# The last norm's token tiles 0 and 1 moved from VectorE to ScalarE and GpSimd

## The chip, the cores and the metric

One NeuronCore of a Trainium2 chip. The metric is the device time of one execution in microseconds (us); before and after are each the median of several runs.

## What is computed

One inference step of a two-layer backbone on 512 latent tokens (`x_sample`) and 128 context tokens (`x_prompt`), 1024 features each. Every layer ends with a squared-ReLU MLP, a gated residual sum and a layer norm; the last of these norms gives the two token outputs:

```python
def layer_norm(x, g, b):
    mu = jnp.mean(xf, -1, keepdims=True)
    var = jnp.mean(jnp.square(xf - mu), -1, keepdims=True)
    return (xf - mu) * lax.rsqrt(var + LN_EPS) * g + b
...
fl = sq_relu_mlp(modulate(xl, ml[3], ml[4]), p["w_up"], p["w_down"])
xl = layer_norm(ALPHA * xl + ml[5] * fl, p["ln2_g"], p["ln2_b"])   # and xc for the prompt
```

## The kernel before

The tokens stand on the partitions in five tiles of 128 (`NT` = 5): tiles 0 to 3 are the latent tokens (`LAT` = 4), tile 4 the prompt. `x[:, t, :]` (named x_tok in the profile) holds tile t as 128x1024 fp32, `acc` a scratch tile of the same shape, `gb` the norm's scale and bias, spread over all partitions, `lnve`, `lnmv` and `lnrs` (ln_small) one or a few numbers per token. Each engine runs its own program in order; semaphores tie them.

The end of the kernel is the last down projection. Its last step makes ten groups, each 12 products of 128x128 by 128x512 into one PSUM bank: `LAST` names them as (half of the features, tile): (0,0), (0,1), (1,0), (1,1), (0,2), (1,2), (0,3), (0,4), (1,3), (1,4). For each group `last_group` (VectorE) multiplies the bank with the gate (one input in PSUM, one in SBUF) and adds the product to `x` (both inputs in SBUF). `LAST_FREE` lets PE reuse a bank only once VectorE's product of an earlier group has been taken: group 8 needs that of group 4, group 9 that of group 5.

When both halves of a latent tile are added, VectorE signals `x_sum`, and `moments` on ScalarE takes the sum of the tile, its negative mean and the sum of the squared deviations (three activations, the first and the last with an accumulator read). `norm_share(3)` on GpSimd scales that sum, adds epsilon and takes the power -0.5 (one element per partition each), which signals `ln_rs`. VectorE applies the norm in two passes per tile, both with two SBUF inputs: `centred` writes (x - mean) * g into `acc`, `final` writes acc * rstd + b into `x` and signals `ln_x`. In the loop over the ten groups they are called for tile 0 after group 4, for tile 1 after group 5, for tile 2 after group 7. After group 9 follow the prompt tile's statistics (`stats`, on VectorE), then `centred(3)`, `centred(4)`, `final(3)` and `final(4)` in two halves. SyncE stores the tiles in the order 0 to 4, each when its `ln_x` has come.

The three norms before this one use `normed` on ScalarE: x * rstd - mean * rstd in place, one activation with `lnrs[:, t, 0:1]` as scale and `lnrs[:, t, 1:2]` as bias.

Of the kernel before, what the change touches and what calls it, by code (L numbers as in the profile page):

```python
# [15 lines left out]
ALU = mybir.AluOpType  # L16
# [6 lines left out]
NT = 5  # L23
LAT = 4
# [88 lines left out]
def build(nc, A, O):  # L113
# [21 lines left out]
    with ctx:  # L135
# [11 lines left out]
        def sem(name):  # L147
            return ctx.enter_context(nc.semaphore(name))
# [10 lines left out]
        x = at("x_tok", 48, [P, NT, D])  # L159
# [6 lines left out]
        gb = at("ln_gb", 184, [P, 2, D])  # L166
# [105 lines left out]
        def two(b, n=HALF):  # L272
# [50 lines left out]
        gb_ld = sem("gb_ld")  # L323
        x_sum, x_mean = sem("x_sum"), sem("x_mean")

        ln_st, ln_rs, ln_n, ln_x, ln_tr, ln_ma, ln_lo = (sem(n) for n in
            ("ln_stat", "ln_rsd", "ln_n", "ln_x", "ln_tr", "ln_ma", "ln_lo"))
# [7 lines left out]
        ic_ld = [sem("ic_ld0"), sem("ic_ld1")]  # L335
        vs, ss_ = sem("dve_step"), sem("pool_step")
        fin, fin2 = sem("stores"), sem("stores_pool")

        (x_prompt, x_sample, cache_k, cache_v, state_ssm, c_in, c_ctx) = (
            A[n] for n in ("x_prompt", "x_sample", "cache_k_l0", "cache_v_l0", "state_ssm_l0", "c", "c_ctx"))  # L340
# [183 lines left out]
        @block.sync  # L524
        def _(sp):
            def load(k, i=None):

                if k == THIRD_K:
                    sp.wait_ge(ib_mm, 8 * NT)
                if k == POOL_K + 1:  # L530
                    sp.wait_ge(acc_ok, DOWNS)
                if k == MIX_K + 2:
                    sp.wait_ge(acc_pre[0], 2)
                if k == w_k[W_OUT[1] + 1]:
                    sp.wait_ge(pl_lo, KT)
                j = raw_before(k)
                if j >= 0 and S[j][0] == "mod":
                    sp.wait_ge(mod_main, m_ord[j] + 1)
                elif j >= 0:
                    sp.wait_ge(lo_done, lin(OPS[w_ord[j] + 1], PER, i))  # L540
                kind, layer, n = S[k]
                if kind == "up":
                    c0 = n * BW if i is None else bass.ds(i * (4 * BW) + n * BW, BW)
                    src = A[f"w_up_l{layer}"][:, slice(c0, c0 + BW) if i is None else c0]
                elif kind == "down":
                    r0 = (n // 2) * CHUNK
                    rows = slice(r0, r0 + CHUNK) if i is None else bass.ds(i * (2 * CHUNK) + r0, CHUNK)
                    src = A[f"w_down_l{layer}"][rows, (n % 2) * 512:(n % 2) * 512 + 512]
                elif kind == "out":
                    src = A[f"w_out_l{layer}"][(n % 2) * 512:(n % 2) * 512 + 512, (n // 2) * 512:(n // 2) * 512 + 512]  # L550
                elif kind == "pool":
                    src = A["pool_w_l1"].rearrange("g k n -> (g k) n")
                elif kind == "mod":
                    src = A[f"w_mod_l{layer}"][:, n * BW:(n + 1) * BW]
                else:
                    src = A[f"w_{kind}_l{layer}"][:, n:n + BW]
                src = src.rearrange("(k p) n -> p k n", p=P)
                sp.dma_start(raw_block(k).rearrange("p (k n) -> p k n", n=src.shape[2]), src) \
                    .then_inc(raw_ld[raw_slot(k)], 16)

            sp.dma_start(head[:], A["t_head"]).then_inc(ld_head, 16)
            sp.dma_start(vec_rows[0:8, 0, :], A["c"].rearrange("a (k p) -> (a k) p", p=P)).then_inc(ld_vec, 16)
            sp.dma_start(vec_rows[8:16, 0, :], A["c_ctx"].rearrange("(k p) -> k p", p=P)).then_inc(ld_vec, 16)
            sp.dma_start(vec_rows[16:56, 0, :], A["conv_w_l0"].rearrange("j (k p) -> (j k) p", p=P)).then_inc(ld_vec, 16)
            sp.dma_start(vec_rows[56:64, 0, :], A["conv_b_l0"].rearrange("(k p) -> k p", p=P)).then_inc(ld_vec, 16)
            sp.dma_start(vec_rows[64:72, 0, :], A["pool_scale_l1"].rearrange("(k p) -> k p", p=P)).then_inc(ld_vec, 16)
            for l in range(2):
                sp.dma_start(vec_rows[48 * l:48 * l + 48, 2, :],
                             A[f"b_mod_l{l}"].rearrange("(k p) -> k p", p=P)).then_inc(ld_vec, 16)
            k = 0  # L570
            for layer in range(2):
                while k < K_UP[layer] + PRE:
                    load(k)
                    k += 1
                with sp.Fori(0, 2) as i:
                    for j in range(BODY):
                        load(k + j, i)
                k += 2 * BODY
            while k < NS:
                load(k)  # L580
                k += 1
            for t in range(LAT):
                sp.wait_ge(ln_x, 3 * NT + t + 1)
                sp.dma_start(y_sample[0, t * P:(t + 1) * P, :], x[:, t, :]).then_inc(fin, 16)
            for n in range(2):
                sp.wait_ge(ln_x, 3 * NT + LAT + n + 1)
                sp.dma_start(y_prompt[0][:, n * 512:(n + 1) * 512], x[:, LAT, n * 512:(n + 1) * 512]).then_inc(fin, 16)
            sp.wait_ge(fin, 16 * (NT + 1))

# [2 lines left out]
        def _(pool):  # L592
# [4 lines left out]
            steps = [0]  # L597
# [91 lines left out]
            def load_gb(i):  # L689
# [3 lines left out]
                for n, which in enumerate("gb"):  # L693
                    pool.dma_start(gb[:, n, :], A[f"ln{half + 1}_{which}_l{layer}"].partition_broadcast(P)) \
                        .then_inc(gb_ld, 16)

            def norm_share(i):

                for t in range(NT):
                    if i == 3 and t < LAT:  # L700
                        pool.wait_ge(x_mean, 3 * t + 3)
                    else:
                        pool.wait_ge(ln_st, NT * i + (t if i < 3 else 0) + 1)
                    if i == 3 and t < LAT:
                        pool.tensor_scalar(lnve[:, t, 1:2], lnve[:, t, 1:2], 1.0 / D, EPS, ALU.mult, ALU.add).then_inc(ss_, 1)
                        steps[0] += 1
                        pool.wait_ge(ss_, steps[0])
                    power = pool.tensor_tensor(lnrs[:, t, 0:1], lnve[:, t, 1:2], halfp[:, 0:1], ALU.pow)
                    if i == 3:
                        power.then_inc(ln_rs, 1)  # L710
                        continue
                    power.then_inc(ss_, 1)
                    steps[0] += 1
                    pool.wait_ge(ss_, steps[0])
                    pool.tensor_tensor(lnrs[:, t, 1:2], lnve[:, t, 0:1], lnrs[:, t, 0:1], ALU.mult).then_inc(ln_rs, 1)

            def spill_x(layer):

# [683 lines left out]
        def _(act):  # L1402
# [472 lines left out]
            def moments(t):  # L1875

                act.wait_ge(x_sum, t + 1)
                act.activation(tmp[:, 0, :], x[:, t, :], ACT.Copy, accum_out=lnmv[:, t, 0:1]).then_inc(x_mean, 1)
                act.wait_ge(x_mean, 3 * t + 1)
                act.activation(lnve[:, t, 0:1], lnmv[:, t, 0:1], ACT.Copy, scale=-1.0 / D).then_inc(x_mean, 1)  # L1880
                act.wait_ge(x_mean, 3 * t + 2)
                act.activation(tmp[:, 1, :], x[:, t, :], ACT.Square, bias=lnve[:, t, 0:1],
                               accum_out=lnve[:, t, 1:2]).then_inc(x_mean, 1)

            for t in range(LAT):
                moments(t)


        @block.vector
        def _(dve):  # L1890
# [513 lines left out]

            def centred(t):

                if t == 0:
                    dve.wait_ge(gb_ld, 32 * 4)
                if t < LAT:
                    dve.wait_ge(x_mean, 3 * t + 2)  # L2410
                else:
                    settle()
                mark(dve.scalar_tensor_tensor(acc[:, t, :], x[:, t, :], lnve[:, t, 0:1], gb[:, 0, :], ALU.add, ALU.mult))

            def final(t):

                dve.wait_ge(ln_rs, NT * 3 + t + 1)
                settle()
                for n in range(2 if t == LAT else 1):
                    cols = slice(n * 512, (n + 1) * 512) if t == LAT else slice(0, D)  # L2420
                    dve.scalar_tensor_tensor(x[:, t, cols], acc[:, t, cols], lnrs[:, t, 0:1], gb[:, 1, cols],
                                             ALU.mult, ALU.add).then_inc(ln_x, 1)
# [127 lines left out]
            def mlp(layer):  # L2550
# [39 lines left out]
                if layer == 1:  # L2590
                    for n in range(2 * NT):
                        last_group(layer, n)
                        if n in (4, 5, 7):
                            centred((4, 5, 7).index(n))
                            final((4, 5, 7).index(n))
                    stats(3, LAT)
                    centred(3)
                    centred(LAT)
                    final(3)
                    final(LAT)  # L2600
                    return
# [139 lines left out]
```

## Time and profile before

| | |
|---|---|
| median of 3 runs | 1454.09 us (1453.24 to 1454.53) |
| the profiled execution, its own time | 1453.4 us |
| its span, first to last instruction | 1451.6 us |
| busy share of the span | PE 96%, VectorE 72%, ScalarE 37%, GpSimd 5% |
| granted TensorE clock, mean | 0.993 of full speed |

In the profile PE is TensorE's products, PEld its weight loads, DVE is VectorE, ACT ScalarE, POOL GpSimd, SP SyncE. A row of the timeline has start in us from the span's start, duration in us, engine, line, operation, output<-inputs, shapes and count; in brackets stands how long the engine was idle before it and what ended that. Rows with a count above 1 are merged neighbours. A start may lie a little before the end of the instruction ahead of it.

### The profile page before, as it was taken

Reading aid. Unit: us, or ns where it says so; the run is one execution under the profiler, and the core shown is the slowest. Engines: PE = TensorE matmul, PEld = TensorE weight load, DVE = VectorE, ACT = ScalarE, POOL = GpSimd, SP = SyncE. Lnnn points to the kernel's source line nnn. Section 1 sums busy time; section 2 is a strip of 40 time slices with the busy share of each in tenths; the row PEclk is TensorE's granted clock in tenths of the full one; section 3 lists DMA queues with packets and bytes.
Section 4 is the critical chain, followed back from the end, with each engine's and each line's share of the span. In section 5 each row is a group of like instructions: output and inputs, shape, how many; then the busy total and the mean of one; then the engine's idle time right before and its main releaser. Section 6 shows DMA issues by size and latency. Waiting matters only on the chain.

```text
span 1451.6 us, 22838 instructions
## 1 busy us (share of the span) xinstructions
PE 1399.1 (96%) x8806; PEld 1241.4 (86%) x8806; DVE 1040.4 (72%) x1651; ACT 543.1 (37%) x982; POOL 77.4 (5%) x146
## 2 busy tenths in 40 slices
PE   4999999899999999999999999999999999999996
PEld 3899988656788998998998879887999899889985
DVE  3694566577568976776776796967887677667778
ACT  3333443267535432332332243434443233223322
POOL 1300000010200000000000111000100000000011
PEclk8999999999999999999999999999999999999998
DMA  9701234496713422312221723551332222123141
GB/s 317 228 30 59 88 118 132 152 333 223 273 58 104 144 60 87 116 59 79 95 87 58 247 82 103 187 194 58 131 116 66 81 87 88 58 87 114 56 163 73
DMA packets 132300, 177.47 MB, mean 122 GB/s; under 512 B 4170, under 2 KB 104258, under 8 KB 131698
## 3 DMA queue, kind: packets, MB, share of 16 engines
q1 hardware_dynamic: 123250, 146.46, 31.5%
q0 software_dynamic: 7376, 26.76, 5.3%
q10 hardware_dynamic: 1584, 3.01, 0.5%
q8 instruction: 61, 1.00, 0.3%
q14 instruction: 29, 0.24, 0.1%
HBM read 166.94 MB, written 9.27 MB: 121 GB/s over the span
## 4 chain that ended last, share of the span: by engine, by line
PE 80%; DVE 10%; ACT 5%; issue 2%; DMA 2%; ACTq 0%; POOL 0%; SPq 0%; DVEq 0%
PE ps L789 40%; PE ps L1307 20%; PE ps L771 6%; PE ps L780 4%; PE ps L820 3%; DVE convT L2002 2%; DVE wlo L1906 1%; PE ps L1115 1%; ACT h_full L1702 1%; DVE p_pad L2669 1%; ACT tmp L1702 1%; ACT whi L1412 1%; PE ps L1126 1%; ACT e_att L1622 1%; DMA raw<-in_w_mod_l 1%
## 5 line engine op out<-in xcount | busy, mean ns | idle before, releaser
L1412 ACT ACTIVATE whi<-raw 128x512 fp32r<-128x512 f32 (+2 forms) x193 | 178.6, 935 | 357.8 <-PE ps L789 293.5
L789 PE MATMUL ps<-whi,hid_hi 128*128 128x512 f32 x640 | 249.6, 390 | 0.0
L789 PE MATMUL ps<-wlo,hid_hi 128*128 128x512 f32 x640 | 249.2, 389 | 0.0
L789 PE MATMUL ps<-whi,hid_lo 128*128 128x512 f32 x640 | 249.0, 389 | 0.0
L1906 DVE TENSOR_TENSOR wlo<-raw,whi 128x512 fp32r<-128x512 f32 (+2 forms) x193 | 204.9, 1070 | 26.0 <-ACT whi L1412 22.5
L2335 DVE TENSOR_TENSOR acc<-acc,ps 128x512 f32<-128x512 f32 x120 | 80.2, 683 | 122.0 <-PE ps L789 122.0
L789 PE MATMUL ps<-whi,h_hi 128*128 128x256 f32 (+1 forms) x480 | 157.4, 328 | 2.4 <-DVE wlo L1906 1.4
L789 PE MATMUL ps<-whi,h_lo 128*128 128x256 f32 (+1 forms) x480 | 152.9, 319 | 0.0
L789 PE MATMUL ps<-wlo,h_hi 128*128 128x256 f32 (+1 forms) x480 | 152.8, 318 | 0.0
L789 PEld LDWEIGHTS ps<-whi,hid_hi 128*128 128x128 f32 x640 | 120.1, 188 | 25.3 <-DVE wlo L1906 0.8
L789 PEld LDWEIGHTS ps<-whi,hid_lo 128*128 128x128 f32 x640 | 120.2, 188 | 25.1
L789 PEld LDWEIGHTS ps<-wlo,hid_hi 128*128 128x128 f32 x640 | 120.1, 188 | 24.3
L1307 PE MATMUL ps<-t_hi,whi 128*128 128x320 f32 x384 | 118.7, 309 | 0.0
L1307 PE MATMUL ps<-t_hi,wlo 128*128 128x320 f32 x384 | 118.7, 309 | 0.0
L1307 PE MATMUL ps<-h_lo,whi 128*128 128x320 f32 x384 | 118.6, 309 | 0.0
L1307 PE MATMUL ps<-h_hi,whi 128*128 128x320 f32 x384 | 118.2, 309 | 0.0
L2475 DVE TENSOR_TENSOR tmp<-tmp,ps 128x320 f32<-128x320 f32 x168 | 79.2, 483 | 37.3 <-PE ps L1307 33.1
L789 PEld LDWEIGHTS ps<-whi,h_hi 128*128 128x128 f32 x480 | 91.2, 190 | 10.7 <-issue 2.3
L789 PEld LDWEIGHTS ps<-whi,h_lo 128*128 128x128 f32 x480 | 91.3, 190 | 6.4
L789 PEld LDWEIGHTS ps<-wlo,h_hi 128*128 128x128 f32 x480 | 91.4, 190 | 5.9
L1307 PE MATMUL ps<-h_hi,wlo 128*128 128x320 f32 x288 | 89.0, 309 | 0.0
L771 PE MATMUL ps<-h_hi,whi 128*128 128x320 f32 x320 | 74.3, 314 | 0.0
(339 smaller groups left out, 2657.2 us busy)
## 6 DMA issues: line engine op xcount, KB each, us to landing
raw<-in_w_up_l SPq DMA_DIRECT2D x32, 1024.0 KB, 5.6
raw<-in_w_down_l SPq DMA_DIRECT2D x32, 1024.0 KB, 5.1
raw<-in_w_mod_l SPq DMA_DIRECT2D x26, 1024.0 KB, 5.4
raw<-in_w_in_l SPq DMA_DIRECT2D x12, 1024.0 KB, 5.3
raw_split<-in_w_mod_l SPq DMA_DIRECT2D x8, 1024.0 KB, 7.2
raw<-in_w_out_l SPq DMA_DIRECT2D x6, 1024.0 KB, 5.7
x_spill<-x_tok POOLq DMA_DIRECT2D x10, 512.0 KB, 2.9
x_tok<-x_spill POOLq DMA_DIRECT2D x10, 512.0 KB, 6.1
```

Of the source, the lines that this page charges most:

```text
L771: mm = pe.matmul(outs[hf], w_of(still, k), a_of(part, k, hf), start=(k == 0 and part == 0 and still == 0), stop=(k == nk - 1 and still == 1))
L780: mm = pe.matmul(out, w_of(still, k), a_of(part, k, hf), start=(k == 0 and part == 0 and still == 0), stop=(k == nk - 1 and still == 1))
L789: mm = pe.matmul(out, a_of(still, k), w_of(part, k), start=(first and k == 0 and part == 0 and still == 0), stop=(last and k == nk - 1 and ...
L820: mm = pe.matmul(ps[32 * g:32 * g + 32, lo:lo + BW], cpad[:, k, :], raw_block(mod_k[m])[:, k * BW:(k + 1) * BW], start=(k < 4), stop=(k >= 4))
L1115: mm = pe.matmul(bank(2 * n + part, 0, keys.shape[-1]), qT[r:r + DH, 2 * n + hp, t * P:(t + 1) * P], keys, start=True, stop=True)
L1307: mm = pe.matmul(bank(b, 0, HALF), WP[still][:, pos // 4, lo:lo + P], moving(part, k), start=(k == 0 and still == 0 and part == 0), stop=( ...
L1412: act.activation(ring_piece(whi, w, g), piece(w, g), ACT.Copy).then_inc(hi_done, 1)
L1702: ins = act.activation(dst, bank(TURN[i % 2][t][f // 4], (f % 4) * P, (f % 4 + 1) * P), ACT.Identity, bias=modT[:, layer, q, f, c:c + 1], ...
L1906: dve.tensor_tensor(ring_piece(wlo, w, g), piece(w, g), ring_piece(whi, w, g).bitcast(F32), ALU.subtract).then_inc(lo_done, 1)
L2002: ins = dve.scalar_tensor_tensor(dst, src, tap, dst, ALU.mult, ALU.add)
L2335: dve.tensor_tensor(dst, dst, bank(4 + g % 4), ALU.add).then_inc(acc_ok, 1)
L2475: dve.tensor_tensor(dst, a, bank(b, 0, HALF), ALU.add).then_inc(comb, 1)
```

## The change

For tiles 0 and 1 of the last norm the two VectorE passes go. ScalarE runs `normed(3, 0)` and `normed(3, 1)` among its moments, and GpSimd, inside `norm_share(3)`, makes the negative mean times rstd for them and multiplies and adds `gb` to the whole tile (`closing`), `closing(0)` behind tile 1's small operations and `closing(1)` behind tile 2's power. The stores of tiles 0 and 1 wait for `y_pool` in place of `ln_x`. Tiles 2, 3 and 4 keep their two VectorE passes.

```diff
             for t in range(LAT):
-                sp.wait_ge(ln_x, 3 * NT + t + 1)
+                if t < 2:
+                    sp.wait_ge(y_pool, t + 1)
+                else:
+                    sp.wait_ge(ln_x, 3 * NT + t - 1)
                 sp.dma_start(y_sample[0, t * P:(t + 1) * P, :], x[:, t, :]).then_inc(fin, 16)
...
+            def closing(t):
+
+                if t == 0:
+                    pool.wait_ge(gb_ld, 32 * 4)
+                pool.wait_ge(ln_n, NT * 3 + t + 1)
+                pool.tensor_tensor(x[:, t, :], x[:, t, :], gb[:, 0, :], ALU.mult).then_inc(ss_, 1)
+                steps[0] += 1
+                pool.wait_ge(ss_, steps[0])
+                pool.tensor_tensor(x[:, t, :], x[:, t, :], gb[:, 1, :], ALU.add).then_inc(y_pool, 1)
...
                     power = pool.tensor_tensor(lnrs[:, t, 0:1], lnve[:, t, 1:2], halfp[:, 0:1], ALU.pow)
-                    if i == 3:
+                    if i == 3 and t >= 2:
                         power.then_inc(ln_rs, 1)
+                        if t == 2:
+                            closing(1)
                         continue
                     power.then_inc(ss_, 1)
                     steps[0] += 1
                     pool.wait_ge(ss_, steps[0])
                     pool.tensor_tensor(lnrs[:, t, 1:2], lnve[:, t, 0:1], lnrs[:, t, 0:1], ALU.mult).then_inc(ln_rs, 1)
+                    if i == 3 and t == 1:
+                        closing(0)
...
-            for t in range(LAT):
-                moments(t)
+            moments(0)
+            moments(1)
+            normed(3, 0)
+            moments(2)
+            normed(3, 1)
+            moments(3)
...
                         last_group(layer, n)
-                        if n in (4, 5, 7):
-                            centred((4, 5, 7).index(n))
-                            final((4, 5, 7).index(n))
+                        if n == 7:
+                            centred(2)
+                            final(2)
```

## Rows read from the trace of the kernel before

**Rows 1.** The page, part 1: busy time, share and instructions of each engine.

```profile
PE 1399.1 (96%) x8806; PEld 1241.4 (86%) x8806; DVE 1040.4 (72%) x1651; ACT 543.1 (37%) x982; POOL 77.4 (5%) x146
```

**Rows 2.** Chain that ended last, 1415 to 1452: start, duration, what.

```profile
1417.06 8.47 PE ps L789 x36
```

**Rows 3.** Timeline of PE, products of the last groups: first and last of 61.

```profile
1425.13 0.39 PE L789 MATMUL ps<-whi,hid_lo 128*128 128x512 f32 x1
...
1438.73 0.39 PE L789 MATMUL ps<-whi,hid_lo 128*128 128x512 f32 x1
```

**Rows 4.** Timeline of VectorE, 1425 to the end.

```profile
1425.56 0.69 DVE L2354 TENSOR_TENSOR gated<-ps,gate 128x512 f32<-128x512 f32 x1 [0.85 <-PE ps L789]
1426.28 0.69 DVE L2357 TENSOR_TENSOR x_tok<-x_tok,gated 128x512 f32<-128x512 f32 x1
1426.89 1.28 DVE L2413 SCALAR_TENSOR_TENSOR acc<-x_tok,ln_small,ln_gb 128x1024 f32<-128x1024 f32 x1
1428.28 1.28 DVE L2421 SCALAR_TENSOR_TENSOR x_tok<-acc,ln_small,ln_gb 128x1024 f32<-128x1024 f32 x1
1429.49 0.68 DVE L2354 TENSOR_TENSOR gated<-ps,gate 128x512 f32<-128x512 f32 x1
...
1433.40 0.69 DVE L2354 TENSOR_TENSOR gated<-ps,gate 128x512 f32<-128x512 f32 x1
...
1437.43 1.28 DVE L2421 SCALAR_TENSOR_TENSOR x_tok<-acc,ln_small,ln_gb 128x1024 f32<-128x1024 f32 x1
...
1440.68 0.69 DVE L2357 TENSOR_TENSOR x_tok<-x_tok,gated 128x512 f32<-128x512 f32 x1
1441.41 1.29 DVE L2367 BATCH_NORM_STATS2 ln_small<-x_tok 128x6 f32<-128x512 f32 x2
...
1443.10 2.59 DVE L2413 SCALAR_TENSOR_TENSOR acc<-x_tok,ln_small,ln_gb 128x1024 f32<-128x1024 f32 x2
1445.80 2.61 DVE L2421 SCALAR_TENSOR_TENSOR x_tok<-acc,ln_small,ln_gb 128x1024 f32<-128x1024 f32 x3
```

**Rows 5.** Tile view of the stored tiles, 1419 to 1452: min/median/max ns, starts.

```profile
L587 SPq DMA_DIRECT2D out<-x_tok x2: 332/332/333, 1447.8 to 1448.4; - x2
DMA to landing us min/median/max: 2.6/2.6/2.7
```

**Rows 6.** Source view of L1687: the earlier norms' `normed`, min/median/max ns.

```profile
L1687 ACT ACTIVATE x_tok<-x_tok,ln_small x15: 1242/1244/1281, 421.8 to 1024.6; 128x1024 f32<-128x1024 f32 x15
```

**Rows 7.** Timeline of ScalarE: start of tile 0's moments, end of tile 1's.

```profile
1423.42 1.06 ACT L1878 ACTIVATE tmp<-x_tok 128x1024 f32<-128x1024 f32 x1 [9.69 <-DVE x_tok L2357]
...
1428.44 0.19 ACT L1882 ACTIVATION_READ_ACCUMULATOR tmp<-x_tok,ln_small 128x1 f32 x1
```

**Rows 8.** GpSimd's groups by form: busy us, mean ns, idle before.

```profile
L745 POOL MEMSET u_pad<- 128x1344 f32 x1 | 1.2, 1222 | 0.0
...
L593 POOL MEMSET cpad<- 128x256 f32 x1 | 0.3, 311 | 0.3 <-POOLq L2727 0.3
```

**Rows 9.** Timeline of GpSimd and VectorE in the first norm, around 444.

```profile
444.38 0.67 POOL L715 TENSOR_TENSOR ln_small<-ln_small 128x1 f32<-128x1 f32 x1
...
444.30 0.69 DVE L2324 SCALAR_TENSOR_TENSOR x_tok<-x_tok,gated 128x512 f32<-128x512 f32 x1
444.91 2.28 DVE L1906 TENSOR_TENSOR wlo<-raw,whi 128x2048 fp32r<-128x2048 f32 x1
```

**Rows 10.** Timeline of GpSimd in the last norm.

```profile
1426.45 0.95 POOL L708 TENSOR_TENSOR ln_small<-ln_small,smisc 128x1 f32<-128x1 f32 x1
1428.72 0.90 POOL L705 TENSOR_SCALAR ln_small<-ln_small 128x1 f32<-128x1 f32 x1 [1.31 <-ACT tmp L1882]
1429.70 0.55 POOL L708 TENSOR_TENSOR ln_small<-ln_small,smisc 128x1 f32<-128x1 f32 x1
1433.68 0.19 POOL L705 TENSOR_SCALAR ln_small<-ln_small 128x1 f32<-128x1 f32 x1 [3.43 <-ACT tmp L1882]
...
1443.10 1.69 POOL L708 TENSOR_TENSOR ln_small<-ln_small,smisc 128x1 f32<-128x1 f32 x2
```

More of the change, by code:

```diff
@@ L337, in build @@
         fin, fin2 = sem("stores"), sem("stores_pool")
+        y_pool = sem("y_pool")
         (x_prompt, x_sample, cache_k, cache_v, state_ssm, c_in, c_ctx) = (
@@ L582, in _ @@
             for t in range(LAT):
-                sp.wait_ge(ln_x, 3 * NT + t + 1)
+                if t < 2:
+                    sp.wait_ge(y_pool, t + 1)
+                else:
+                    sp.wait_ge(ln_x, 3 * NT + t - 1)
                 sp.dma_start(y_sample[0, t * P:(t + 1) * P, :], x[:, t, :]).then_inc(fin, 16)
             for n in range(2):
-                sp.wait_ge(ln_x, 3 * NT + LAT + n + 1)
+                sp.wait_ge(ln_x, 3 * NT + LAT + n - 1)
                 sp.dma_start(y_prompt[0][:, n * 512:(n + 1) * 512], x[:, LAT, n * 512:(n + 1) * 512]).then_inc(fin, 16)
@@ L2405, in centred @@
             def centred(t):
-                if t == 0:
+                if t == 2:
                     dve.wait_ge(gb_ld, 32 * 4)
```

## The prediction

> **What bounds the kernel now.** I read the busy line and the last link of PE's work first: PE is busy for 96% of the span [rows 1], so nothing that VectorE saves ahead of PE's last product is worth anything, and only the end of the run is open to this edit. Then the chain that ended last, for the stretch in which it leaves PE: it runs on PE until 1425.5 and on VectorE from there to the end [rows 2]. Then the timeline, engine by engine.
>
> PE's last product ends at 1438.73 + 0.39 = 1439.12 [rows 3]. Each of the ten last groups is 12 products, and the 60 from 1425.13 to 1438.73 give 0.227 each, so a group comes every 2.72. VectorE took group 4 at 1425.56, having waited 0.85 for PE [rows 4]; so the groups are ready for it at 1425.56, 1428.28, 1431.00, 1433.72, 1436.44 and 1439.16. It doesn't follow that beat: the two passes over tile 0 (`centred` at 1426.89, `final` at 1428.28) push group 5 to 1429.49 [rows 4], 1.2 behind PE, and with those of tiles 1 and 2 the add of group 9 starts at 1440.68 and ends at 1441.37 [rows 4]. Without any of these passes group 9 would be taken at 1439.16 and its add would end at 1440.57 (0.69 + 0.03 + 0.69). So VectorE's lateness behind PE is worth 0.80 us at most. Behind that add everything is serial on VectorE: statistics of the prompt tile from 1441.41, two `centred` from 1443.10, three `final` pieces from 1445.80 [rows 4], and the last store issued at 1448.4, landing 2.7 later [rows 5]. The edit leaves this tail as it is, 10.2 us behind the last add.
>
> **The change, part by part.** All the steps are put on the time line of before, and the sum is how far the end of group 9's add moves from 1441.37.
>
> *Removed from VectorE:* two passes on tiles 0 and 1. From the start of `centred` at 1426.89 to the next group at 1429.49 a pair takes 2.60 [rows 4], so 5.2 us of work goes. By the 0.80 above at most 0.8 of it can show: the rest was cover for waiting on PE.
>
> *Added to ScalarE:* two `normed` of 1.244 [rows 6]. ScalarE's `moments` of tile 0 runs from 1423.42, and tile 1's ends at 1428.44 + 0.19 = 1428.63 [rows 7]; then `normed(0)` runs to 1429.85. `moments(2)` can't start before group 5's add ends (1428.28 + 1.41 = 1429.69), so it runs 1429.8 to 1432.4 (2.6, half of the 5.21 that two took), and `normed(1)` to 1433.65. This is hidden: before, the scale behind tile 2's moments began as late as 1433.68 [rows 10].
>
> *Added to GpSimd:* a small multiply for tiles 0 and 1 (0.2 to 0.7, like the one at 444.38 [rows 9]), and in `closing(0)` and `closing(1)` four 128x1024 operations with two SBUF inputs. GpSimd is in order, so tile 2's `power`, on which VectorE's `final(2)` waits, now stands behind `closing(0)`, and those of tiles 3 and 4 behind `closing(1)`. No row of before has a wide GpSimd operation with inputs. The nearest are its memsets: 1.222 for 1344 elements and 0.311 for 256 [rows 8], 0.84 ns an element, so 0.95 for 1024 that are only written: the lower bound. If two reads and a write pass one after another it is three times that, less two starts of 0.1: about 2.7, the upper bound. Two reads in turn with the write beneath give 1.8. I take the middle of the last two, 2.25, because each of the streams needs at least the memset's time and something is lost in joining them. The Trainium skill (GPSIMD Engine Reference, 3.1 Elementwise) has 4497 ns for 2048 elements of such an add; half of it is 2.25, and no run here shows it yet.
>
> *The wait between the two engines.* GpSimd's one-element operations show a pattern [rows 9, 10]. The multiply at 444.38 took 0.67, and ended 0.06 behind VectorE's 444.30 + 0.69, an operation with both inputs in SBUF. The scale at 1428.72 took 0.90 and ended at 1429.62, 0.06 behind the end of `final` (1429.56), again two SBUF inputs. The scale at 1433.68 took 0.19, though VectorE was at work, on a group's product with one input in PSUM (from 1433.40 [rows 4]). So there is a way into SBUF which a two-input VectorE operation needs, and GpSimd stands still for the whole of it. I assume the other direction too: a wide GpSimd operation that holds it makes VectorE's two-input operations wait to its end. The rows can't show that, since GpSimd's operations there need the way only for one element. The multiply at 444.38 also shows who is next: the second VectorE operation (444.91, two inputs) was queued as well and GpSimd still got in between, so I let the two engines alternate.
> The Trainium skill (SBUF — State Buffer, Who interferes with whom) says the same of both directions: a VectorE operation with two SBUF inputs and a GpSimd one that reads SBUF exclude each other, the first to issue keeps the shared pair and the other fully blocks. It speaks against this edit: by it the sum below is +4.2, with only the direction that the rows show it is -0.6.
>
> The working, with 2.25 for a wide operation:
> - `power` and multiply of tile 1, ready from 1428.63, finish between 1429.9 and 1430.4, as its `power` meets group 5's add (1429.00 to 1429.69) or not; `closing(0)` multiply 1430.2 to 1432.45.
> - VectorE group 6: product 1431.00 to 1431.69, its add (two inputs) wants 1431.72, gets 1432.45, ends 1433.14.
> - `closing(0)` add: 1433.14 to 1435.39.
> - Group 7: product 1433.72 to 1434.41; add gets 1435.39, ends 1436.08. `centred(2)` 1436.00 to 1437.28 (1.28).
> - GpSimd: scale of tile 2 slips in at 1436.1, `power` waits for `centred(2)` and ends 1437.28 + 0.43 = 1437.71 (0.43 is what the `power` at 1426.45, 0.95 long, took beyond the add that ended at 1426.97 [rows 4, 10]).
> - Now `final(2)` and `closing(1)`'s multiply want the way at once. GpSimd's next instruction needs no signal from another engine, so I give it the turn: 1437.8 to 1440.05. `final(2)` 1440.05 to 1441.33.
> - `closing(1)` add 1441.33 to 1443.58. Group 8: product done by 1441.94, add 1443.58 to 1444.27. Group 9: product 1444.19 to 1444.88, add 1444.91 to 1445.60.
>
> 1445.60 - 1441.37 = **+4.2 us**. Group 8's product starts at 1441.25, 4.8 after PE was done with it. Behind it no wide GpSimd operation is left. The `power` of tiles 3 and 4 keeps its place: before, both were done (1443.10 + 1.69 = 1444.79 [rows 10]) 1.0 ahead of `final(3)`, and they hang on the same adds as before. Stores: tile 1's starts at 1443.7 and tile 2's right behind it, in the same queue; at 2.6 to 2.7 to landing each, both are through before tile 3's (1451.4) and cost nothing. PE isn't touched: its groups 8 and 9 need the banks of groups 4 and 5, freed long before.
> The profiled execution took 1453.4 with a span of 1451.6; that becomes 1457.6. The median of the runs is 0.7 above that execution, so 1454.1 + 4.2 = **1458.3**.
>
> With the operation's time the sum moves about fourfold, for all four stand in the chain: at 1.8 the same working gives +2.4, at 1.9 about +2.9, at 2.7 +6.0. At the memset's 0.95 nearly everything fits into PE's beat, and it gives +0.3.
>
> **Rivals.**
> - *VectorE wins the turn at 1437.8.* `final(2)` runs to 1439.03, `closing(1)` multiply to 1441.28, group 8's add to 1441.97, the last GpSimd add to 1444.22, group 9's add to 1444.91: +3.5, 1457.6. Close to the forecast in kind; no row measures who wins when both become ready together.
> - *VectorE doesn't wait for GpSimd* (not slower). Its adds go through, GpSimd alone waits: `closing(0)` ends at 1434.8, scale at 1435.18, `power` behind `centred(2)` at 1436.75, `final(2)` to 1438.1, and group 9's add ends at 1440.8: -0.6, 1453.5. For it: no row shows VectorE held. Against it: each row of the other direction shows waiting for the whole, no sharing. It decides as soon as an add of VectorE beside a wide operation keeps its 0.69. A quick wide operation (under 1.9) gives "no change" too, +0.3 to +2.9.
> - *Wide operations longer than 2.7*, since each takes its inputs in turn and the engine's program costs something per element. At 3.2 the fourfold gives +8, 1462. Nothing in the profile speaks for it but that small operations of this engine aren't quick (0.55 for one element of `power`).
>
> **How the numbers follow.** Under 0.2% (2.9 us) this kernel's runs can't be told from no change. Held in both directions with 1.9 to 2.7 per wide operation, either winner of the turn: 0.62 (slower). Longer than that: 0.07 (slower). Held but quick: 0.13 (same). VectorE not held: 0.16 (same). Faster by 2.9 us would need more than the 0.8 that VectorE's lateness is worth, so 0.02 for what I haven't seen. That makes 0.02, 0.29, 0.69. The range reaches down to the case without holding, 1453.5, which also takes in the 0.95 bound, and up to 1460.3 for 2.7. The likeliest case's own range is 1457.0 to 1460.3.
>
> **What would show it.** In the changed profile: four L7xx GpSimd operations of 128x1024, start to start about 2.3 or more; VectorE adds of groups 6 to 9 with gaps ahead of them or lengths above 0.69, ending with a GpSimd operation; `final(2)` around 1440 in place of 1437.43; group 9's add ending near 1445.6, and 10.2 us of tail behind it, unchanged. PE's last product stays at 1439.1 beside the start. Wrong would be: adds at 0.69 on PE's beat (no holding), a wide operation well off 2.25, or `power` of tiles 3 or 4 finishing behind `centred(4)`, which would lengthen the tail as well.

## The result and the profile after

The median went from 1453.99 us (18 runs, 1452.54 to 1457.06) to 1457.85 us (18 runs, 1456.22 to 1458.99): ratio 1.0025, 95% interval 1.0019 to 1.0031, so by the ratio about 3.6 us slower (2.8 to 4.5); the two medians differ by 3.86. That is clear of zero, though the interval just reaches below the 2.9 us under which the prediction wouldn't have told it from no change. The profiled execution took 1456.9 us with a span of 1455.1, 3.5 above the one of before in both.

Timeline of PE after, its last product; start, duration:

```profile
1438.80 0.39 PE L807 MATMUL ps<-whi,hid_lo 128*128 128x512 f32 x1
```

PE ends at 1439.19, against 1439.12 before [rows 3]: all of the difference but 0.07 arises behind it. Timeline of VectorE after, which answers to [rows 4]:

```profile
1428.35 0.69 DVE L2376 TENSOR_TENSOR gated<-ps,gate 128x512 f32<-128x512 f32 x1 [1.30 <-PE ps L807]
...
1431.79 1.16 DVE L2379 TENSOR_TENSOR x_tok<-x_tok,gated 128x512 f32<-128x512 f32 x1
1433.79 0.69 DVE L2376 TENSOR_TENSOR gated<-ps,gate 128x512 f32<-128x512 f32 x1 [0.83 <-PE ps L807]
1434.51 1.25 DVE L2379 TENSOR_TENSOR x_tok<-x_tok,gated 128x512 f32<-128x512 f32 x1
1435.68 1.27 DVE L2435 SCALAR_TENSOR_TENSOR acc<-x_tok,ln_small,ln_gb 128x1024 f32<-128x1024 f32 x1
1437.40 3.39 DVE L2443 SCALAR_TENSOR_TENSOR x_tok<-acc,ln_small,ln_gb 128x1024 f32<-128x1024 f32 x1 [0.44 <-POOL ln_small L722]
1440.71 0.68 DVE L2376 TENSOR_TENSOR gated<-ps,gate 128x512 f32<-128x512 f32 x1
1441.43 2.11 DVE L2379 TENSOR_TENSOR x_tok<-x_tok,gated 128x512 f32<-128x512 f32 x1
...
1444.17 0.69 DVE L2379 TENSOR_TENSOR x_tok<-x_tok,gated 128x512 f32<-128x512 f32 x1
1444.90 1.29 DVE L2389 BATCH_NORM_STATS2 ln_small<-x_tok 128x6 f32<-128x512 f32 x2
...
1449.30 2.61 DVE L2443 SCALAR_TENSOR_TENSOR x_tok<-acc,ln_small,ln_gb 128x1024 f32<-128x1024 f32 x3
```

and the timeline of GpSimd after, which answers to [rows 10]:

```profile
1429.99 2.42 POOL L706 TENSOR_TENSOR x_tok<-x_tok,ln_gb 128x1024 f32<-128x1024 f32 x1
1432.48 2.73 POOL L709 TENSOR_TENSOR x_tok<-x_tok,ln_gb 128x1024 f32<-128x1024 f32 x1
1435.30 0.52 POOL L719 TENSOR_SCALAR ln_small<-ln_small 128x1 f32<-128x1 f32 x1
1435.90 1.47 POOL L722 TENSOR_TENSOR ln_small<-ln_small,smisc 128x1 f32<-128x1 f32 x1
1437.34 2.38 POOL L706 TENSOR_TENSOR x_tok<-x_tok,ln_gb 128x1024 f32<-128x1024 f32 x1
1439.79 3.20 POOL L709 TENSOR_TENSOR x_tok<-x_tok,ln_gb 128x1024 f32<-128x1024 f32 x1
```

A held operation shows no idle time: it shows as too long. The two views have to be read side by side, ends against ends. (The end of a row is its start plus its duration.) VectorE's add of group 6 (L2379 at 1431.79) took 1.16 in place of 0.69 and ended 0.54 behind GpSimd's multiply (1432.41). Group 7's took 1.25 and ended 0.55 behind GpSimd's add (1435.21). `final(2)` (L2443) took 3.39 in place of 1.28 and ended 1.07 behind the next multiply (1439.72), and group 8's add took 2.11 and ended 0.55 behind the last GpSimd add (1442.99). In turn GpSimd's adds took 2.73 and 3.20 where its multiplies took 2.42 and 2.38, and its `power` took 1.47, ending 0.42 behind `centred(2)` (1436.95). The products with one input in PSUM (L2376) kept 0.68 to 0.69 all along. Group 9's add ends at 1444.86, 3.5 later than before.

### The profile page after: what moved, and what is told of

It is laid out like the page before. It is cut to its first block, busy times and chain, and to the rows that moved or that the text cites. A ratio compares the mean times of both kernels' runs of the same rounds, so it can differ in the third digit from the quotient of the medians.

```text
span 1455.1 us, 22841 instructions
## 1 busy us (share of the span) xinstructions
PE 1399.0 (96%) x8806; PEld 1241.4 (85%) x8806; DVE 1040.6 (72%) x1647; ACT 545.4 (37%) x984; POOL 89.0 (6%) x152
## 4 chain that ended last, share of the span: by engine, by line
PE 78%; DVE 11%; ACT 5%; issue 3%; DMA 1%; POOL 1%; ACTq 0%; SPq 0%; DVEq 0%; POOLq 0%
PE ps L807 38%; PE ps L1325 20%; PE ps L789 6%; PE ps L798 4%; PE ps L838 3%; DVE convT L2024 2%; DVE wlo L1928 2%; PE ps L1133 1%; ACT h_full L1720 1%; DVE p_pad L2691 1%; ACT whi L1430 1%; DVE acc L2365 1%; PE ps L1144 1%; ACT tmp L1720 1%; ACT e_att L1640 1%
```

## The experiments

**How they are read.** PE's last product ended anywhere from 1439.1 to 1443.4 in the ten traces. No edit did that: the whole spread is there 300 us ahead of anything edited (the same product of PE starts at 1100.30 in before and at 1104.58 in e8_one_tile). That the traces of before and after agree to 0.07 in PE's end is chance, and the wobble is larger than most differences looked for. So besides the ratio I give the stretch from the end of PE's last product to the end of VectorE's last operation. Before: 1445.80 + 2.61 - 1439.12 = 9.3. After: 1451.91 - 1439.19 = 12.7. The expectations of e5, e6, e8 and e9 use the same stretch up to the end of the span, 12.5 and 15.9; those of e1 to e4 give times as if PE ended where it did in after. Each ratio is to runs of before made alongside (medians 1454.36 for e1 to e4, 1455.36 for the others).

| kernel | ratio to before, 95% interval | PE's end to VectorE's end, us | to the span's end, us |
|---|---|---|---|
| before | | 9.3 | 12.5 |
| after | 1.0025 (1.0019 to 1.0031) | 12.7 | 15.9 |
| e1_write_only | 0.9999 (0.9990 to 1.0008) | 8.6 | 11.8 |
| e2_no_wide | 0.9997 (0.9988 to 1.0006) | 8.5 | 11.7 |
| e3_powers_first | 1.0037 (1.0023 to 1.0051) | 14.8 | 18.0 |
| e4_psum | 0.9995 (0.9986 to 1.0004) | 8.6 | 11.8 |
| e5_before_psum | 1.0000 (0.9991 to 1.0009) | 9.3 | 12.5 |
| e6_scalar_only | 1.0003 (0.9994 to 1.0012) | 10.6 | 13.7 |
| e8_one_tile | 1.0000 (0.9991 to 1.0009) | 9.2 | 12.3 |
| e9_psum_early_stats | 0.9999 (0.9990 to 1.0008) | 8.8 | 13.4 |

By the ratio only after and e3_powers_first differ from before. The intervals of all the others include 1 and end at 1.0012 or lower, below after's 1.0019: that their loss is gone is shown by the times. The finer differences, such as the 0.7 and 0.8 us under before, stand on one trace each.

### e2_no_wide: without the wide operations

```diff
-                pool.tensor_tensor(x[:, t, :], x[:, t, :], gb[:, 0, :], ALU.mult).then_inc(ss_, 1)
...
-                pool.tensor_tensor(x[:, t, :], x[:, t, :], gb[:, 1, :], ALU.add).then_inc(y_pool, 1)
+                pool.memset(acc[:, t, 0:1], 0.0).then_inc(y_pool, 1)
```

> The kernel after without the four wide GpSimd operations (the scale and bias of tiles 0 and 1 are left out); ScalarE's two normed stay. Both theories: VectorE follows PE, group 9's add ends near 1440.6, span about 1450.9, 4.2 below after and 0.7 below before (ratio 0.9995). If ScalarE's or the small GpSimd operations cost something by themselves, it stays above 1451.6.

Timeline of VectorE in this kernel, the add of group 9:

```profile
1440.18 0.69 DVE L2376 TENSOR_TENSOR x_tok<-x_tok,gated 128x512 f32<-128x512 f32 x1
```

Group 9's add ended at 1440.87 and the span was 1451.1. The stretch fell by 0.8 against before, the whole of what VectorE's lateness behind PE could give. So ScalarE's two passes and the small operations cost nothing, and all of the loss sits in the four wide operations.

### e1_write_only: GpSimd as busy, but reading nothing

```diff
-                pool.tensor_tensor(x[:, t, :], x[:, t, :], gb[:, 0, :], ALU.mult).then_inc(ss_, 1)
+                pool.memset(acc[:, 0:2, :], 0.0).then_inc(ss_, 1)
+                steps[0] += 1
+                pool.wait_ge(ss_, steps[0])
+                pool.memset(acc[:, 0, 0:640], 0.0).then_inc(ss_, 1)
...
(the same two in place of the add)
```

> The kernel after, but each of the four wide GpSimd operations is replaced by two memsets of scratch (128x2048 and 128x640, about 2.5 us together by the memset rows), so GpSimd is occupied as long and at the same place but reads nothing from SBUF; the scale and bias of tiles 0 and 1 are left out. Theory (VectorE's two-input operations are held by GpSimd operations that read): the adds of groups 6 to 9 keep 0.69, final(2) keeps 1.28 and runs from about 1436.9, group 9's add ends near 1440.9 in place of 1444.86, span about 1451.1, ratio to before 0.9997. Rival (the cost is that tile 2's power queues behind closing(0), or that GpSimd is simply occupied): group 9's add ends near 1444.9 and the span stays near 1455.

Timelines of VectorE and GpSimd in this kernel, around `final(2)`:

```profile
1438.41 1.28 DVE L2449 SCALAR_TENSOR_TENSOR x_tok<-acc,ln_small,ln_gb 128x1024 f32<-128x1024 f32 x1 [0.45 <-POOL ln_small L728]
...
1440.33 0.69 DVE L2385 TENSOR_TENSOR x_tok<-x_tok,gated 128x512 f32<-128x512 f32 x1
...
1436.95 1.43 POOL L728 TENSOR_TENSOR ln_small<-ln_small,smisc 128x1 f32<-128x1 f32 x1
1438.33 1.81 POOL L706 MEMSET acc<- 128x2048 f32 x1
1440.20 0.63 POOL L709 MEMSET acc<- 128x640 f32 x1
```

`final(2)` ran beside a memset for the whole of its 1.28, where it took 3.39 beside the multiply. The `power`, 1.43 long, ends 0.41 behind `centred(2)`, as in after (0.42), and VectorE waits for it as long (0.45 and 0.44). So GpSimd's being occupied, with tile 2's `power` queued behind it, costs next to nothing: the stretch is 8.6, within 0.2 of that without wide operations. It is the reading that holds VectorE.

### e3_powers_first: tile 2's power out of the queue

```diff
                         if t == 2:
+                            closing(0)
                             closing(1)
...
-                    if i == 3 and t == 1:
-                        closing(0)
```

> The kernel after, with tile 2's scale and power ahead of closing(0), so that VectorE never waits for a number from GpSimd; closing(0) and closing(1) follow back to back. Theory (held in both directions, engines in turn): four operations of 2.4 alternate with group 7's add, centred(2), final(2) and group 8's add; group 9's add ends near 1447.0, span near 1457.2, 2 us ABOVE after (ratio to before 1.0038). Rival (the lateness of tile 2's power is the cost): the power is done by 1433.4, final(2) starts at 1436.4, span about 1450.9, as without the wide operations.

Timelines of VectorE and GpSimd in this kernel:

```profile
1434.54 1.77 DVE L2378 TENSOR_TENSOR x_tok<-x_tok,gated 128x512 f32<-128x512 f32 x1
1436.23 3.42 DVE L2434 SCALAR_TENSOR_TENSOR acc<-x_tok,ln_small,ln_gb 128x1024 f32<-128x1024 f32 x1
1439.76 3.17 DVE L2442 SCALAR_TENSOR_TENSOR x_tok<-acc,ln_small,ln_gb 128x1024 f32<-128x1024 f32 x1
...
1443.56 2.12 DVE L2378 TENSOR_TENSOR x_tok<-x_tok,gated 128x512 f32<-128x512 f32 x1
...
1432.85 0.55 POOL L722 TENSOR_TENSOR ln_small<-ln_small,smisc 128x1 f32<-128x1 f32 x1
1433.36 2.40 POOL L706 TENSOR_TENSOR x_tok<-x_tok,ln_gb 128x1024 f32<-128x1024 f32 x1
1435.84 2.73 POOL L709 TENSOR_TENSOR x_tok<-x_tok,ln_gb 128x1024 f32<-128x1024 f32 x1
1438.52 3.33 POOL L706 TENSOR_TENSOR x_tok<-x_tok,ln_gb 128x1024 f32<-128x1024 f32 x1
1441.92 3.20 POOL L709 TENSOR_TENSOR x_tok<-x_tok,ln_gb 128x1024 f32<-128x1024 f32 x1
```

The `power` is done by 1433.40, 4 us earlier than in after, and the kernel is slower by another 2.1 (span 1457.2, as forecast; group 9's add ends at 1447.00). Taking away the wait for the number only moved the wide operations to where VectorE has four operations with two SBUF inputs and just one product between them, and each of those is held once: 1.77, 3.42, 3.17, 2.12. The rival, lateness of the number, falls.

### e4_psum and its control: VectorE off the shared way

```diff
-                dve.tensor_tensor(pg[:, n % 2, :], bank(LAST_BANK[n]), gate[:, 0, int(t == LAT), cols],
+                part = bank(n % 2) if layer == 1 else pg[:, n % 2, :]
+                dve.tensor_tensor(part, bank(LAST_BANK[n]), gate[:, 0, int(t == LAT), cols],
...
-                ins = dve.tensor_tensor(x[:, t, cols], x[:, t, cols], pg[:, n % 2, :], ALU.add)
+                ins = dve.tensor_tensor(x[:, t, cols], x[:, t, cols], part, ALU.add)
...
+                dst = ps[:, 1024:2048] if t == 2 else acc[:, t, :]
...
+                    src = ps[:, 1024:2048] if t == 2 else acc[:, t, cols]
```

`centred` writes `dst`, `final` reads `src`.

> The kernel after, full computation, but the gated product of each last group and centred(2)'s result are written to PSUM banks 0 to 3, free by then, in place of SBUF: the adds and final(2) have one SBUF input. Theory (only operations with two SBUF inputs are held): the adds of groups 6 to 9 keep about 0.69 beside the wide GpSimd operations and final(2) about 1.28; only centred(2) can still be held; group 9's add ends near 1440.9, span near 1451.1, ratio to before 0.9997. Rival (GpSimd slows or holds VectorE whatever it reads, or the queue is the cost): span stays 1454.5 to 1455.5.

Timelines of VectorE and GpSimd in this kernel:

```profile
1433.06 0.69 DVE L2380 TENSOR_TENSOR x_tok<-x_tok,ps 128x512 f32<-128x512 f32 x1
...
1438.10 1.28 DVE L2446 SCALAR_TENSOR_TENSOR x_tok<-ps,ln_small,ln_gb 128x1024 f32<-128x1024 f32 x1 [0.43 <-POOL ln_small L722]
...
1440.03 0.69 DVE L2380 TENSOR_TENSOR x_tok<-x_tok,ps 128x512 f32<-128x512 f32 x1
...
1431.24 2.42 POOL L706 TENSOR_TENSOR x_tok<-x_tok,ln_gb 128x1024 f32<-128x1024 f32 x1
1433.73 2.41 POOL L709 TENSOR_TENSOR x_tok<-x_tok,ln_gb 128x1024 f32<-128x1024 f32 x1
...
1438.04 2.41 POOL L706 TENSOR_TENSOR x_tok<-x_tok,ln_gb 128x1024 f32<-128x1024 f32 x1
1440.52 2.36 POOL L709 TENSOR_TENSOR x_tok<-x_tok,ln_gb 128x1024 f32<-128x1024 f32 x1
```

Each of these VectorE rows overlaps a wide GpSimd one, and neither side is stretched: adds 0.69, `final(2)` 1.28, all four wide operations 2.36 to 2.42. The full computation is done, the same work on the same engines as in after, and the 3.4 us and another 0.7 are back. `centred(2)`, which still has two SBUF inputs, met no wide operation here.

> The kernel before with the gated products and tile 2's centred result in PSUM, as in e4_psum: the control for it. Theory: nothing wide runs on GpSimd, so nothing is held that PSUM could free; the stretch from PE's last product to the end stays 12.5, ratio 1.0000. Rival (PSUM operands are themselves quicker and e4_psum's gain came from that): below 12.0.

The same edit in the kernel before left the stretch at 9.3, so operands in PSUM are not quicker by themselves. What they bring in e4_psum is that GpSimd's reads no longer hold VectorE.

### e8_one_tile and e6_scalar_only: the change in parts

```diff
                 pool.wait_ge(ln_n, NT * 3 + t + 1)
+                if t == 1:
+                    pool.memset(acc[:, t, 0:1], 0.0).then_inc(y_pool, 1)
+                    return
```

> The kernel after without closing(1)'s two wide operations (the scale and bias of tile 1 are left out); closing(0) stays where it is. Read from the end of PE's last product, which moves from run to run by itself: before takes 12.5 us from there to the end of the span, after 15.9. Theory (each operation held behind a wide GpSimd operation pays for it, but only from group 7 on is there no slack before PE): closing(0)'s holds are absorbed by VectorE's waits for PE; tile 2's power still comes after closing(0) and centred(2), final(2) keeps 1.28; the stretch is 12.4 to 12.5, so closing(1) alone carries the whole 3.4 (ratio to before 1.0000). Rival (both closings share the cost): about 14.2, ratio 1.0012.

Timeline of VectorE in this kernel, the add of group 6 and group 7:

```profile
1435.99 1.16 DVE L2382 TENSOR_TENSOR x_tok<-x_tok,gated 128x512 f32<-128x512 f32 x1
1437.99 0.69 DVE L2379 TENSOR_TENSOR gated<-ps,gate 128x512 f32<-128x512 f32 x1 [0.83 <-PE ps L810]
1438.71 1.25 DVE L2382 TENSOR_TENSOR x_tok<-x_tok,gated 128x512 f32<-128x512 f32 x1
```

The adds of groups 6 and 7 took 1.16 and 1.25, held by `closing(0)` just as in after, yet the stretch is 9.2, before's. VectorE waits 1.3 for PE ahead of group 6 and only 0.83 ahead of group 7: the hold on group 6 was paid out of that slack. The hold on group 7 and the later `power` are paid out of the 0.8 that the removed passes had given. `closing(1)` runs where VectorE has no slack left: taking it away brings back 3.5, the whole of the loss. That is its price behind `closing(0)`; what it would cost alone was not run.

```diff
+            def scaled(t):
...
+                dve.wait_ge(ln_n, 3 * NT + t + 1)
+                mark(dve.tensor_tensor(x[:, t, :], x[:, t, :], gb[:, 0, :], ALU.mult))
+                settle()
+                dve.tensor_tensor(x[:, t, :], x[:, t, :], gb[:, 1, :], ALU.add).then_inc(ln_x, 1)
...
+                        if n in (5, 6):
+                            scaled(n - 5)
```

> ScalarE's part alone, full computation: tiles 0 and 1 are normalised by ScalarE as in after, their scale and bias applied by VectorE in two passes (1.22 each), tile 0 behind group 5 and tile 1 behind group 6, no wide GpSimd operation. Theory: nothing is held, all two-input operations keep their lengths; but VectorE does two passes of 1.22 in place of two of 1.28 and starts them 2.7 us later than before, so that tile 1's run 1433.75 to 1436.2 and group 9's add ends near 1442.8: stretch from PE's end 13.9 (before 12.5, after 15.9), ratio to before 1.0010. Rival (ScalarE's normed itself costs, or saves): all of after's 15.9, or below 12.5.

No VectorE operation was held, and the stretch was 10.6 (13.7 to the span's end), 1.3 more than before, nearly as forecast. With no wide GpSimd operation ScalarE's part gains nothing: VectorE still makes two passes a tile, 1.22 to 1.23 in place of 1.28, and later. By the ratio it can't be told from before.

### e9_psum_early_stats: trying for a version that beats both

```diff
                             centred(2)
+                            stats(3, LAT, (0,))
                             final(2)
...
-                    stats(3, LAT)
+                    stats(3, LAT, (1,))
```

This comes on top of e4_psum's edit; `stats` now takes the halves that it is to do.

> A version meant to be the best, full computation: e4_psum, and the first half of the prompt tile's statistics taken ahead of final(2), into the 0.43 us in which VectorE waits there for GpSimd's power. Theory: final(2) moves 0.35 later, group 9's add too, and one 0.6 us pass leaves the tail: stretch from PE's last product to the end 11.5 (before 12.5, e4_psum 11.75), ratio to before 0.9993. Rival (the wait isn't free because VectorE is the bound there): 11.75, no gain over e4_psum.

Timelines of VectorE and GpSimd in this kernel, around `final(2)` and in the tail:

```profile
1440.26 0.69 DVE L2390 BATCH_NORM_STATS2 ln_small<-x_tok 128x6 f32<-128x512 f32 x1
1441.06 1.28 DVE L2448 SCALAR_TENSOR_TENSOR x_tok<-ps,ln_small,ln_gb 128x1024 f32<-128x1024 f32 x1
...
1446.14 2.60 DVE L2439 SCALAR_TENSOR_TENSOR acc<-x_tok,ln_small,ln_gb 128x1024 f32<-128x1024 f32 x2
1449.18 2.61 DVE L2448 SCALAR_TENSOR_TENSOR x_tok<-acc,ln_small,ln_gb 128x1024 f32<-128x1024 f32 x3 [0.44 <-POOL ln_small L722]
...
1446.45 1.01 POOL L719 TENSOR_SCALAR ln_small<-ln_small 128x1 f32<-128x1 f32 x1 [1.03 <-ACT tmp L1900]
1447.55 2.11 POOL L722 TENSOR_TENSOR ln_small<-ln_small,smisc 128x1 f32<-128x1 f32 x2
```

The theory failed here: the stretch to VectorE's end is 8.8, no better than e4_psum. "No gain" is what the rival said, but its reason is not what the trace shows: `final(2)` came 0.4 later, about as the theory itself had reckoned, and the pass did leave the tail. But the two `centred` then started before tile 3's scale could get in, held it (1.01 in place of 0.19) and then the `power`, and `final(3)` waited 0.44 for the number. It is the other direction of the same hold, and these 0.44 are what the theory had left out. The 13.4 to the span's end holds a further wait of SyncE for PE's queue at the program's end, 1.8 where the others have 0.2 to 0.3; its cause is open. So e4_psum stays the best full computation by the traces. Its ratio is 0.5 in a thousand under before, with an interval that includes no change; only the trace tells it from before.

## Why the prediction was right

- *Where it could show.* Right: e2_no_wide gave the 0.8 that VectorE's lateness was said to be worth, and nothing ahead of PE's end took part.
- *ScalarE and the small operations hidden.* Right: `normed(0)` ran 1428.61 to 1429.84, `normed(1)` 1432.40 to 1433.63.
- *A wide operation at 2.25.* Measured 2.38 to 2.42 unheld (start to start 2.49 and 2.45), inside the bounds 0.95 to 2.7. I had taken the middle between two ways of joining the reads and the write, 1.8 and 2.7, and no run tests either: that it lies so near is in part luck. The Trainium skill (GPSIMD Engine Reference, 3.1 Elementwise) gives 4497 ns for 2048 elements; the estimate from it, half of that, is 2.25 as well, about 6% below these rows.
- *Held in both directions.* The step that the trace of before could not show. Right by the trace of after and by three runs that each gave the theory's number: 1.28 kept beside writes (e1), 1457.2 with the number early (e3), nothing stretched with one input in PSUM (e4). This is what the Trainium skill states (SBUF — State Buffer, Who interferes with whom), one that only writes being exempt by it as well, and these traces agree: 3.39 beside a read, 1.28 beside a memset.
- *In turn, GpSimd first at the tie.* Right: its multiply is recorded at 1437.34, `final(2)` at 1437.40, and it took the way. The rival in which VectorE wins it didn't occur in this trace. Its sum, +3.5, is what was measured, but that is a coincidence: the order of the rows is the other one. Who wins was seen at this one place only.
- *The sum.* +4.2 forecast, +3.5 in the profiled execution, 3.6 by the ratio. The working put the chain too late, by a little at most steps: 1444.79 for group 9's add (less the 0.07 of PE) against 1445.60. The mis-sized term is what a held operation still needs once the way is free. I gave it its whole length, 0.69 and 1.28; it needs 0.54 to 0.55 and 1.07. Four of those are 0.6 less. The earlier start (1429.92, again less the 0.07, for 1430.2) and the longer multiplies (2.42 and 2.38 for 2.25) cancel; most of the rest is the gap of 0.09 that I had put ahead of `closing(1)`'s multiply and that isn't there. Two sums beside it were slightly off: by the fourfold rule 1.9 gives +2.8, not +2.9, and 2.7 gives 1460.1, not 1460.3.
- *The tail unchanged.* Right: from the end of group 9's add to the end of the span 10.2 both times.

## What to carry to other kernels

Before giving GpSimd elementwise work, look at what VectorE does beside it. If VectorE's operations have both inputs in SBUF and GpSimd's read SBUF, in these traces the two engines take turns by whole instructions, and the work isn't moved but added, at 2.4 us for 1024 fp32 elements instead of 1.2. It is free only where VectorE waits for something else, or where one of VectorE's inputs can be put in PSUM: here that edit took back all of the loss. And in these traces a hold shows as a longer instruction, not as idle time, so a view of waits doesn't name it.

## What the runs showed of the hardware that was not expected

- A held VectorE operation ends 0.54 to 0.56 (128x512) or 1.07 to 1.08 (128x1024) behind the GpSimd one, in after and in e3_powers_first, less than its 0.69 and 1.28. So 0.13 to 0.21 of its length is not needed after the release; which part that is, no row shows.
- GpSimd's wide operation, when held, needed 2.26 and 2.20 from there (1432.95 to 1435.21, 1440.79 to 1442.99) against 2.38 to 2.42 unheld.
- The end of PE's last product wandered by 4.3 us over ten traces, with the mean granted clock at 0.991 to 0.994. Of the 4.3 between before and e8_one_tile 2.7 are there at the product at 1013.65 (1016.38) and all at the one at 1100.30 (1104.58). What it comes from was not followed further.
